# Block 2's mixers: the value projection of each head pair one pair later

## The chip, the cores and the metric

The kernel runs on one core of one Trainium2 chip. The metric is the device time of one execution in microseconds (us). Before the change it is 3103.43 us, the median of three runs (3101.84 to 3103.62).

## The reference, cut to what matters

Two blocks of two layers each work on a stream of 512 tokens of width 1024 in f32. The change concerns the mixers of the second block: in each, one projection gives queries, keys and values, 8 pairs of heads attend, and an output projection follows.

```python
def dilated_attention_mixer(u, w_in, w_out, cos, sin):          # block 2, layer 0: "mixer 1"
    q, k, v = jnp.split(u @ w_in, 3, axis=-1)
    q = apply_partial_rope(split_heads(q, A_HEADS), cos, sin)   # 16 heads of 64: 8 head pairs
    k = apply_partial_rope(split_heads(k, A_HEADS), cos, sin)
    v = split_heads(v, A_HEADS)
    ...
        o, lse = banded_attention(by_residue(q)[..., None, :, :], by_residue(k), by_residue(v),
                                  radius, A_BLOCK)
    ...
    w = jax.nn.softmax(jnp.stack(lses), axis=0)
    o = jnp.einsum('pbhs,pbhsd->bhsd', w, jnp.stack(outs))
    return merge_heads(o).astype(u.dtype) @ w_out

def differential_attention_mixer(u, w_in, w_out, lam_q1, ..., sub_g, cos, sin, layer_idx):   # layer 1: "mixer 2"
    q, k, v = jnp.split(u @ w_in, 3, axis=-1)
    ...
        p = jax.nn.softmax(sc, axis=-1)
        a = p[:, :, 0] - lam * p[:, :, 1]
        return jnp.einsum('bhqk,bhkd->bhqd', a.astype(v.dtype), v, preferred_element_type=f32)
    ...
    o = rms_norm(o, sub_g) * (1.0 - lam_init)
    return merge_heads(o).astype(u.dtype) @ w_out
```

A pair of heads (two of 64 in mixer 1, the two halves of one head in mixer 2) needs 128 columns of q, of k and of v: 24 column tiles in all.

## The kernel before, in words

All is written out by hand: each engine has its own program, and semaphores tie them together. A **unit** is one column tile of a weight, 1024 x 128, times all 512 tokens. SyncE loads its weight in the order of the list `stream()`, ScalarE makes `w_hi` of it (L1470), VectorE the rest `w_lo` (L2194), four units ahead at most (`SLOTS`), and TensorE then runs 8 x 3 matmuls (L569: hi by hi, lo by hi, hi by lo). In the mixers a unit is cut into two **halves** of 12 matmuls (`half(0)`, `half(1)`), which stand between the steps of the attention.

The function `fused(l)` is the mixer, and exists once for each engine; l is 0 for mixer 1 and 1 (`diff`) for mixer 2. The units come as q0 k0 v0, q1 k1 v1, ... Pass r of the loop (1 to 8) does the attention of pair r-1 while it projects pair r; the last pass has nothing to project. In a pass, for each of four blocks of 128 queries:

- `score(p, q)` (L1139), TensorE: two scores of 512 keys. It waits until the exponentials of the score before it are done, and score 0 until q and k of its pair have been rotated (`f_roped`).
- `maxima` (L2800 in mixer 1, L2798 in mixer 2), VectorE; `exps` (L1974), ScalarE; `normalise` (L2808 to L2817), VectorE.
- `turn(p, q)` (L1150), TensorE: the probabilities transposed; `copies` (L1983), ScalarE.
- `values(r)` (L1172), TensorE: the pair's v, evicted to `y`, is transposed into bank `F_R`; ScalarE copies it to `v` (L2014).
- `outputs(p)` (L1164, L1160 in mixer 2), TensorE: probabilities times v, one pass later; `take` (L2821), VectorE, brings them to `o`.

The rotation of the next pair's q and k is spread over the pass: `evict` (L2786, L2788), `rope_sin` (L2827, L2829: a shuffle through the same bank `F_R`, times the sine), the product with the cosine on GpSimd (L3123), and `rope_add` (L2835).

Where TensorE would have nothing to do, `kept_busy` (L596) issues matmuls whose result nobody reads: six in pass 1 and groups of three in the last pass. In the last pass the output projection begins as well (`out_begun`, L569, into banks 0 and 1): its operand `a_hi`, `a_lo` is made of `o` by ScalarE (`out_rounded`, L1830) and VectorE (`out_low`, L2239). Mixer 2 first applies a norm to `o`: `norm_spread` (L1214), TensorE, into banks 0 and 1, free once all 24 units are evicted, and `norm_applied` (L2855), VectorE.

Of the kernel before, what the change touches and what calls it, by code (L numbers as in the profile page):

```python
# [26 lines left out]
P = 128  # L27
# [50 lines left out]

def stream():

    order, at = [], 0
    for _ in range(LAYERS):
        order += [(at + j, 8) for j in range(WIN_T + 8)]
        order += [(at + WIN_T + 72, 0), (at + WIN_T + 76, 0)]
        order += [(at + WIN_T + 8 + j, 8) for j in range(64)]
        order += [(at + WIN_T + 80 + j, 8) for j in range(8)]
        at += WIN_T + 88
    for _ in range(LAYERS):
        order += [(at + 8 * part + r, 8) for r in range(8) for part in range(3)]
        order += [(at + 24 + j, 8) for j in range(8 + 16 + 8 + 8 + 24 + 24 + 12)]  # L90
        order += [(at + 124 + j, 6) for j in range(8)]
        at += 132
    return order
# [110 lines left out]
def build(nc, dram, out):  # L204
    ctx = ExitStack()
    with ctx:
# [268 lines left out]
        def _(pe):  # L475
# [632 lines left out]
            def fused(l):  # L1108
# [59 lines left out]
                def values(r):  # L1168
                    pe.wait_ge(bank_free, first + 3 * r + 3)
                    pe.wait_ge(f_sin, 2 * (pairs + r + 1) + (1 if r + 1 < PAIRS else 0))  # L1170
# [55 lines left out]
                for r in range(1, PAIRS + 1):  # L1226
                    more = r < PAIRS
                    if more:
                        half(0)
                    if r == 1:  # L1230
                        kept_busy(F_O, 6, 2 * P)
                    score(r - 1, 0)
                    if r >= 2:
                        outputs(r - 2)
                    if more:
                        half(1)
                    score(r - 1, 1)
                    turn(r - 1, 0)
                    if more:
                        half(0)  # L1240
                    else:
                        kept_busy(W_BANK[0] if diff else F_R, 3, 2 * P)
                    score(r - 1, 2)
                    if not more and diff:
                        norm_spread(0)
                        norm_spread(1)
                    turn(r - 1, 1)
                    if more:
                        half(1)
                    else:  # L1250
                        kept_busy(F_R, 3, 2 * P)
                    score(r - 1, 3)
                    if not more:
# [3 lines left out]
                        else:  # L1257
                            kept_busy(F_R, 3, 2 * P)
                            out_begun((0, 1))
                    turn(r - 1, 2)  # L1260
                    values(r - 1)
                    if more:
                        half(0)
                    elif diff:
                        pe.wait_ge(f_copied, turns(l, PAIRS) - 2)
                        kept_busy(F_T[1], 4, 2 * P)
                        norm_spread(4)
                        norm_spread(5)
                        kept_busy(F_T[1], 1, 2 * P)
                    else:  # L1270
                        out_begun((2, 3))
# [3 lines left out]
                    if more:  # L1275
# [180 lines left out]
        def _(act):  # L1456
# [505 lines left out]
            def fused(l):  # L1962
# [60 lines left out]
                for r in range(1, PAIRS + 1):  # L2023
                    last = r == PAIRS
                    ahead(first + 3 * r + 2 if not last else first + 3 * r + 1)
                    exps(r - 1, 0)
                    if not last:
                        ahead(first + 3 * r + 3)
# [8 lines left out]
                    else:  # L2037
                        ahead(first + 3 * r + 4)
# [3 lines left out]
                    values(r - 1)  # L2042
# [139 lines left out]
        def _(dve):  # L2182
# [594 lines left out]
            def fused(l):  # L2777
# [45 lines left out]
                def rope_sin(r, k):  # L2823
                    if k == 1 and r > 0:
                        dve.wait_ge(f_v_ready, pairs + r)
# [46 lines left out]
                for r in range(1, PAIRS + 1):  # L2872
                    more = r < PAIRS
                    if more:
                        ahead(first + 3 * r + 2)
# [5 lines left out]
                    normalise(r - 1, 0)  # L2881
                    if r >= 2:
                        take(r - 2)
                    if more:
                        evict(r, 0)
                    maxima(r - 1, 1)
                    if more:
                        ahead(first + 3 * r + 3)
# [4 lines left out]
                    maxima(r - 1, 2)  # L2893
                    if more:
# [16 lines left out]
                    if more:  # L2911
                        rope_sin(r, 1)
                        ahead(first + 3 * r + 4)
                        rope_add(r, 1)
                        evict(r, 2)
# [341 lines left out]
```

## Time and profile before

| | us |
|---|---|
| median of three runs | 3103.43 |
| the profiled execution | 3101.19 |
| its span | 3099.4 |
| TensorE busy with matmuls | 3042.0 (98%) |
| VectorE busy | 1754.2 (57%) |
| ScalarE busy | 1254.4 (40%) |
| GpSimd busy | 297.7 (10%) |

Mixer 1's eight passes run from 1430.92 to about 1657 us of the span, mixer 2's from 2271.61 to about 2503 us. The share of a busy engine is an average over the whole span; what a pass waits for is read in its own timeline, where a row in square brackets says how long the engine stood idle and what released it.

### The profile page before, as it was taken

What the parts mean: (1) busy time and instruction counts of PE and PEld (TensorE: products, weight loads), DVE (VectorE), ACT (ScalarE), POOL (GpSimd) and SP (SyncE); (2) the same over time, 40 slices, a digit from 0 to 9 for tenths busy, and PEclk for the clock granted to TensorE, in tenths of its full rate; (3) what the DMA queues carried; (4) which work ended last, traced back from release to release, by engine and by line L of the source; (5) the groups of instructions that cost most, each with busy time, mean ns of one, the idle gap of its engine ahead of it and who ended that gap; (6) DMA issues with size and microseconds to landing.
All of it is one profiled execution on the core that took longest, in us unless ns stands there. A gap on an engine that the chain in (4) does not pass through costs nothing.

```text
span 3099.4 us, 38484 instructions
## 1 busy us (share of the span) xinstructions
PE 3042.0 (98%) x15248; PEld 2422.4 (78%) x15248; DVE 1754.2 (57%) x2564; ACT 1254.4 (40%) x2084; POOL 297.7 (10%) x257
## 2 busy tenths in 40 slices
PE   7999999999999999999999999999999999999998
PEld 6777888887777888887667878888866678788886
DVE  7755644357656544467775635344577755354444
ACT  6644323245544322344444534232344444342322
POOL 2011100011011100011001102000110010020001
PEclk9999999999999999999999999999999999999999
DMA  3111233332111333332112322233211133223332
GB/s 139 55 49 60 93 100 95 95 96 86 56 42 66 95 96 101 95 95 74 55 55 89 122 68 82 95 98 100 89 60 56 48 95 112 65 89 97 101 95 82
DMA packets 73726, 259.14 MB, mean 84 GB/s; under 512 B 8020, under 2 KB 10200, under 8 KB 73176
## 3 DMA queue, kind: packets, MB, share of 16 engines
q1 hardware_dynamic: 72824, 252.99, 26.1%
q0 software_dynamic: 736, 3.87, 0.4%
q8 instruction: 113, 1.85, 0.2%
q14 instruction: 53, 0.43, 0.0%
HBM read 254.73 MB, written 2.10 MB: 83 GB/s over the span
## 4 chain that ended last, share of the span: by engine, by line
PE 84%; issue 6%; DVE 6%; ACT 1%; POOLq 1%; DVEq 1%; DMA 0%; POOL 0%; ACTq 0%
PE bank L569 68%; PE bank L499 2%; PE bank L1139 1%; POOLq L3081 1%; PE bank L793 1%; DVE w_lo L2194 1%; PE bank L1150 1%; PE bank L1364 1%; PE bank L1343 1%; PE bank L1094 1%; PE bank L1160 1%; PE bank L1164 1%; PE bank L823 0%; PE bank L836 0%; DMA w_raw<-weights 0%
## 5 line engine op out<-in xcount | busy, mean ns | idle before, releaser
L569 PE MATMUL bank<-a_hi,w_hi 128*128 128x512 f32 x2120 | 848.1, 400 | 19.3 <-DVE w_lo L2194 15.1
L569 PE MATMUL bank<-a_hi,w_lo 128*128 128x512 f32 x2120 | 828.6, 391 | 0.0
L569 PE MATMUL bank<-a_lo,w_hi 128*128 128x512 f32 x2120 | 827.4, 390 | 0.0
L2194 DVE TENSOR_TENSOR w_lo<-w_raw,w_hi 128x1024 fp32r<-128x1024 f32 (+1 forms) x474 | 612.2, 1293 | 285.4 <-ACT w_hi L1470 283.7
L1470 ACT ACTIVATE w_hi<-w_raw 128x1024 fp32r<-128x1024 f32 (+1 forms) x474 | 494.8, 1045 | 417.1 <-DMA w_raw<-weights 417.1
L569 PE MATMUL bank<-b_hi,w_hi 128*128 128x512 f32 (+1 forms) x1516 | 572.9, 378 | 2.6 <-DVE w_lo L2194 1.5
L569 PE MATMUL bank<-b_lo,w_hi 128*128 128x512 f32 (+1 forms) x1516 | 564.2, 372 | 0.0
L569 PE MATMUL bank<-b_hi,w_lo 128*128 128x512 f32 (+1 forms) x1516 | 564.0, 372 | 0.0
L569 PEld LDWEIGHTS bank<-a_hi,w_hi 128*128 128x128 f32 x2120 | 399.3, 188 | 120.0 <-issue 21.7
L569 PEld LDWEIGHTS bank<-a_hi,w_lo 128*128 128x128 f32 x2120 | 399.0, 188 | 85.6
L569 PEld LDWEIGHTS bank<-a_lo,w_hi 128*128 128x128 f32 x2120 | 399.6, 189 | 83.2 <-issue 3.8
L569 PEld LDWEIGHTS bank<-b_hi,w_hi 128*128 128x128 f32 x1516 | 286.2, 189 | 63.4 <-issue 9.7
L569 PEld LDWEIGHTS bank<-b_hi,w_lo 128*128 128x128 f32 x1516 | 286.3, 189 | 50.2
L569 PEld LDWEIGHTS bank<-b_lo,w_hi 128*128 128x128 f32 x1516 | 286.5, 189 | 49.9 <-issue 1.7
L3080 POOL TENSOR_TENSOR sq_sum<-sq_sum,sq 128x512 f32<-128x512 f32 (+1 forms) x119 | 160.6, 1349 | 322.1 <-ACT sq L1523 317.7
L1974 ACT ACTIVATE prob<-bank,der 128x512 f32<-128x512 f32 x128 | 87.0, 685 | 207.8 <-DVE der L2800 108.4
L3078 POOL COPY sq_sum<-sq 128x512 f32<-128x512 f32 (+1 forms) x18 | 11.5, 639 | 1580.9 <-ACT sq L1523 1580.9
L2604 DVE TENSOR_TENSOR x<-x,bank 128x512 f32<-128x512 f32 x80 | 55.0, 687 | 179.6 <-PE bank L569 179.6
L1867 ACT ACTIVATE y<-y 128x512 f32<-128x512 f32 x64 | 40.4, 632 | 219.7 <-DVE y L2642 219.7
L2140 ACT ACTIVATE b_hi<-y 128x512 fp32r<-128x512 f32 x44 | 27.8, 632 | 189.1 <-DVE y L3033 189.1
L3039 DVE TENSOR_TENSOR y<-y,bank 128x512 f32<-128x512 f32 x46 | 31.6, 688 | 119.1 <-PE bank L569 119.1
L2239 DVE TENSOR_TENSOR b_lo<-y,b_hi 128x512 fp32r<-128x512 f32 x76 | 52.7, 693 | 69.7 <-ACT b_hi L1868 39.0
(341 smaller groups left out, 3172.5 us busy)
## 6 DMA issues: line engine op xcount, KB each, us to landing
w_raw<-weights SPq DMA_DIRECT2D x458, 512.0 KB, 3.5
w_raw<-weights SPq DMA_DIRECT2D x16, 384.0 KB, 3.0
x<-x SPq DMA_DIRECT2D x8, 256.0 KB, 7.4
mem<-mem POOLq DMA_DIRECT2D x2, 1024.0 KB, 5.3
out<-x SPq DMA_DIRECT2D x8, 256.0 KB, 2.1
mem<-mem SPq DMA_DIRECT2D x1, 1024.0 KB, 12.4
ple<-ple POOLq DMA_DIRECT2D x2, 512.0 KB, 4.0
o<-c_level SPq DMA_DIRECT2D x1, 512.0 KB
```

The source lines that it names most:

```text
L499: last = mm(bank[unit_bank(u) if at is None else at][:, hs(e)], w[:, u % SLOTS, ks], t[:, k, hs(e)], start=(k == 0 and n == 0), stop=(k == ...
L569: last = mm(bank[unit_bank(u) if at is None else at][:, 0:cols], w[:, u % SLOTS, ks], t[:, k, 0:cols], start=(k == begun and n == 0), stop ...
L793: last = mm(bank[2 + 2 * p + e][:, cols], k_, q_, start=True, stop=True)
L1094: last = mm(bank[b][:, :], w[:, u % SLOTS, ks], t[:, k, :], start=(k == 0 and i == 0), stop=(k == 1 and i == 2))
L1470: f(w_hi[:, u % SLOTS, 0:widths[u]], w_raw[:, u % SLOTS, 0:widths[u]], ACT.Copy).then_inc(w_hi_ready, 1)
L1867: f(y[:, 20 + j % 2, :], y[:, 16 + j % 2, :], ACT.Square)
L1974: f(prob[:, i % 4, :], bank[F_S[e]][:, :], ACT.Exp, bias=stat_n[:, i % 8:i % 8 + 1], scale=1.0 if diff else -1.0, accum_out=stat_d[:, i % ...
L2194: tt(w_lo[:, u % SLOTS, w], w_raw[:, u % SLOTS, w], f32(w_hi[:, u % SLOTS, w]), ALU.subtract).then_inc(w_lo_ready, 1)
L2239: tt(h[1][:, k, :], src, f32(h[0][:, k, :]), ALU.subtract).then_inc(h_ready, 1)
L2604: tt(x[:, k, :], x[:, k, :], b[:, :], ALU.add).then_inc(bank_free, 1)
L3039: step(lambda u, b: tt(y[:, k, :], y[:, k, :], b[:, :], ALU.add).then_inc(bank_free, 1))
L3080: pool.tensor_tensor(sq_sum[:, 0:cols], sq_sum[:, 0:cols], s, ALU.add).then_inc(sq_added, 1)
```

## The change

In both mixers q and k keep their places, and each v but the first is projected one pass later: the order becomes q0 k0 v0, q1 k1, q2 k2 v1, ..., q7 k7 v6, v7. Pass 1 projects q1, k1 and the first half of q2, and pass 2 begins with its score at once, without a half ahead of it. The last pass has the two halves of v7. `values` moves from the end of its pass to the place behind the first score of the next, `outputs` from behind the first score to behind the second, `take` from ahead of the second maxima to behind them. Of the groups of three `kept_busy` matmuls in the last pass, two go in mixer 1 and two in mixer 2; in mixer 2 the first two `norm_spread` now come behind the second turn. The weight splits (`ahead`) of pass 1 become one fewer and the last pass has one more.

```diff
@@ the order of the weights
+MIX_ORDER = [(0, 0), (1, 0), (2, 0), (0, 1), (1, 1)]
+MIX_ORDER += [u for r in range(2, 8) for u in ((0, r), (1, r), (2, r - 1))] + [(2, 7)]
...
-        order += [(at + 8 * part + r, 8) for r in range(8) for part in range(3)]
+        order += [(at + 8 * part + r, 8) for part, r in MIX_ORDER]
...
@@ TensorE
                 def values(r):
-                    pe.wait_ge(bank_free, first + 3 * r + 3)
-                    pe.wait_ge(f_sin, 2 * (pairs + r + 1) + (1 if r + 1 < PAIRS else 0))
+                    pe.wait_ge(bank_free, first + MIX_ORDER.index((2, r)) + 1)
+                    pe.wait_ge(f_sin, 2 * (pairs + min(r + 2, PAIRS)))
+                    if r == PAIRS - 1:
+                        pe.wait_ge(f_v_ready, pairs + r)
...
                 for r in range(1, PAIRS + 1):
                     more = r < PAIRS
-                    if more:
+                    if r == 1:
                         half(0)
-                    if r == 1:
                         kept_busy(F_O, 6, 2 * P)
+                    elif r > 2 and more:
+                        half(0)
                     score(r - 1, 0)
                     if r >= 2:
+                        values(r - 2)
+                    half(1 if more else 0)
+                    score(r - 1, 1)
+                    if r >= 2:
                         outputs(r - 2)
-                    if more:
-                        half(1)
-                    score(r - 1, 1)
                     turn(r - 1, 0)
-                    if more:
-                        half(0)
-                    else:
-                        kept_busy(W_BANK[0] if diff else F_R, 3, 2 * P)
+                    half(0 if more else 1)
                     score(r - 1, 2)
-                    if not more and diff:
-                        norm_spread(0)
-                        norm_spread(1)
                     turn(r - 1, 1)
                     if more:
                         half(1)
+                    elif diff:
+                        norm_spread(0)
+                        norm_spread(1)
                     else:
+                        pe.wait_ge(f_v_ready, pairs + PAIRS - 1)
                         kept_busy(F_R, 3, 2 * P)
                     score(r - 1, 3)
...
-                            kept_busy(F_R, 3, 2 * P)
                             out_begun((0, 1))
                     turn(r - 1, 2)
-                    values(r - 1)
                     if more:
                         half(0)
...
                     turn(r - 1, 3)
-                    if more:
+                    if more and r > 1:
                         half(1)
...
@@ ScalarE
-                    ahead(first + 3 * r + 2 if not last else first + 3 * r + 1)
+                    ahead(first + (5 if r == 1 else 3 * r + 1))
                     exps(r - 1, 0)
+                    if r >= 2:
+                        values(r - 2)
                     if not last:
-                        ahead(first + 3 * r + 3)
+                        ahead(first + (6 if r == 1 else 3 * r + 2))
...
@@ VectorE
                 def rope_sin(r, k):
-                    if k == 1 and r > 0:
-                        dve.wait_ge(f_v_ready, pairs + r)
+                    if k == 0 and r > 1:
+                        dve.wait_ge(f_v_ready, pairs + r - 1)
...
                     normalise(r - 1, 0)
+                    if more:
+                        evict(r, 0)
+                    maxima(r - 1, 1)
                     if r >= 2:
                         take(r - 2)
                     if more:
-                        evict(r, 0)
-                    maxima(r - 1, 1)
-                    if more:
-                        ahead(first + 3 * r + 3)
+                        ahead(first + (6 if r == 1 else 3 * r + 2))
                     normalise(r - 1, 1)
...
                     maxima(r - 1, 2)
+                    if not more:
+                        evict(r - 1, 2)
...
                         rope_sin(r, 1)
-                        ahead(first + 3 * r + 4)
+                        if r > 1:
+                            ahead(first + 3 * r + 3)
                         rope_add(r, 1)
-                        evict(r, 2)
+                        if r > 1:
+                            evict(r - 1, 2)
```

Three places show the new order. Line numbers of the changed kernel are 4 higher on TensorE up to L1150, where they were, 6 higher behind it, and 8 higher on VectorE. The first place is TensorE at the end of pass 1 of mixer 1; L569 or L573 and a line of dots is a half of 12 matmuls (in the last but one row before, of 24). Before:

```order
L1139 MATMUL bank<-y 128x512 x2
L1150 MATMUL bank<-small,prob 128x128 x8
L1172 MATMUL bank<-small,y 128x128 x4
L569 MATMUL bank<-a_hi,w_hi 128x512
...
L1150 MATMUL bank<-small,prob 128x128 x8
L569 MATMUL bank<-a_hi,w_hi 128x512
...
L1139 MATMUL bank<-y 128x512 x2
L1164 MATMUL bank<-prob_t,v 64x512 x8
```

And now:

```order
L1143 MATMUL bank<-y 128x512 x2
L1154 MATMUL bank<-small,prob 128x128 x8
L573 MATMUL bank<-a_hi,w_hi 128x512
...
L1154 MATMUL bank<-small,prob 128x128 x8
L1143 MATMUL bank<-y 128x512 x2
L1178 MATMUL bank<-small,y 128x128 x4
```

The last turn of pass 1 (L1154) and the first score of pass 2 (L1143) are now neighbours, where two halves lay between, and the transposed values (L1178) stand behind that score.

The second place is TensorE in the last pass of mixer 2, from the second score on (L1150 is a turn, L596 the `kept_busy` group, L1214 two `norm_spread`). Before:

```order
L1139 MATMUL bank<-y 128x512 x2
L1150 MATMUL bank<-small,prob 128x128 x4
L596 MATMUL bank<-small 128x256 x3
L1139 MATMUL bank<-y 128x512 x2
L1214 MATMUL bank<-small,g_r 128x128 x8
L1150 MATMUL bank<-small,prob 128x128 x4
L596 MATMUL bank<-small 128x256 x3
L1139 MATMUL bank<-y 128x512 x2
L1214 MATMUL bank<-small,g_r 128x128 x8
L1150 MATMUL bank<-small,prob 128x128 x4
L1172 MATMUL bank<-small,y 128x128 x4
```

And now (the half in it is the second of v7):

```order
L1143 MATMUL bank<-y 128x512 x2
L1164 MATMUL bank<-prob_t,v 128x512 x4
L1154 MATMUL bank<-small,prob 128x128 x4
L573 MATMUL bank<-a_hi,w_hi 128x512
...
L1143 MATMUL bank<-y 128x512 x2
L1154 MATMUL bank<-small,prob 128x128 x4
L1220 MATMUL bank<-small,g_r 128x128 x8
L1143 MATMUL bank<-y 128x512 x2
L1220 MATMUL bank<-small,g_r 128x128 x8
L1154 MATMUL bank<-small,prob 128x128 x4
L1178 MATMUL bank<-small,y 128x128 x4
```

Both groups of three are gone, a half stands in the place of the first, and the first spreads come behind the turn and right ahead of the fourth score.

The third place is VectorE in the same pass (L2821 is `take`, L2840 the clamp of the norm, L2798 maxima, L2855 two `norm_applied`). Before:

```order
L2821 COPY o<-bank 128x512
L2798 TENSOR_REDUCE der<-bank 128x1 x2
L2808 RECIPROCAL der<-der 128x2
L2812 TENSOR_SCALAR prob<-prob,der 128x512
L2814 SCALAR_TENSOR_TENSOR prob<-prob,der 128x512
L2840 TENSOR_SCALAR y<-o 128x512
L2798 TENSOR_REDUCE der<-bank 128x1 x2
L2855 SCALAR_TENSOR_TENSOR o<-bank,vec,o 128x512 x2
```

And now:

```order
L2806 TENSOR_REDUCE der<-bank 128x1 x2
L2829 COPY o<-bank 128x512
L2816 RECIPROCAL der<-der 128x2
L2820 TENSOR_SCALAR prob<-prob,der 128x512
L2822 SCALAR_TENSOR_TENSOR prob<-prob,der 128x512
L2848 TENSOR_SCALAR y<-o 128x512
L2806 TENSOR_REDUCE der<-bank 128x1 x2
L2796 TENSOR_TENSOR y<-bank,r_x 128x512
L2863 SCALAR_TENSOR_TENSOR o<-bank,vec,o 128x512 x2
```

The copy of the outputs stands behind the maxima, and the eviction of v7 (L2796) ahead of the norm.

## Rows read from the trace of the kernel before

**Rows 1.** The page, sections 1 and 5: busy us; a group: busy us, mean ns, idle.

```profile
PE 3042.0 (98%) x15248; PEld 2422.4 (78%) x15248; DVE 1754.2 (57%) x2564; ACT 1254.4 (40%) x2084; POOL 297.7 (10%) x257
...
L2194 DVE TENSOR_TENSOR w_lo<-w_raw,w_hi 128x1024 fp32r<-128x1024 f32 (+1 forms) x474 | 612.2, 1293 | 285.4 <-ACT w_hi L1470 283.7
```

**Rows 2.** TensorE's waits: line, releaser, us in total, times, longest.

```profile
PE bank L1139 <- DVE y L2835: 2.1, 3, 1.1
...
PE bank L569 <- DVE o L2855: 0.8, 1, 0.8
```

**Rows 3.** Pass 2, mixer 1; passes 2 and 8, mixer 2: stretch, length, busy, clock.

```profile
1456.25:1485.13 28.88, 28.88 (x141) 19.23 (x140) 20.34 (x43) 13.14 (x28) 2.59 (x2) 1.00 0.18 56
...
2296.26:2324.47 28.21, 27.95 (x125) 18.83 (x124) 21.72 (x36) 11.99 (x26) 2.60 (x2) 1.00 0.18 55
...
2463.21:2502.82 39.61, 36.49 (x173) 24.30 (x173) 24.04 (x47) 16.70 (x36) 0.59 (x1) 1.00 0.12 41
```

**Rows 4.** Timeline, mixer 1, passes 1 and 2: start, us, engine, line; idle before.

```profile
1446.62 0.60 PE L1172 MATMUL bank<-small,y 128*128 128x128 f32 x4
...
1449.83 1.04 PE L1150 MATMUL bank<-small,prob 128*128 128x128 f32 x8
...
1456.25 1.13 PE L1139 MATMUL bank<-y 64*128 64x512 f32 x4
...
1460.89 0.50 PE L569 MATMUL bank<-a_hi,w_hi 128*128 128x512 f32 x1
...
1461.01 0.69 DVE L2821 COPY o<-bank 128x512 f32<-128x512 f32 x1 [0.20 <-PE bank L1164]
...
1463.84 1.13 PE L1139 MATMUL bank<-y 64*128 64x512 f32 x4
```

**Rows 5.** Timeline, VectorE and GpSimd, end of pass 1, mixer 1: the rotation.

```profile
1450.09 1.29 POOL L3123 TENSOR_TENSOR y<-y,cos_t 128x512 f32<-128x512 f32 x1 [5.54 <-DVE bank L2827]
...
1450.71 1.75 DVE L2194 TENSOR_TENSOR w_lo<-w_raw,w_hi 128x1024 fp32r<-128x1024 f32 x1
1452.38 0.68 DVE L2835 TENSOR_TENSOR y<-y,f_t 128x512 f32<-128x512 f32 x1
```

**Rows 6.** Timeline, TensorE, last pass of mixer 1.

```profile
1633.48 1.46 PE L596 MATMUL bank<-small 128*128 128x256 f32 x6
...
1638.40 1.13 PE L1139 MATMUL bank<-y 64*128 64x512 f32 x4
...
1641.65 0.47 PE L569 MATMUL bank<-a_hi,w_hi 128*128 128x512 f32 x1 [0.64 <-DVE a_lo L2239]
```

**Rows 7.** Timeline, TensorE and GpSimd, passes 1 and 2 of mixer 2.

```profile
2290.19 0.66 PE L1150 MATMUL bank<-small,prob 128*128 128x128 f32 x4 [0.48 <-DVE prob L2814]
...
2291.03 1.30 POOL L3123 TENSOR_TENSOR y<-y,cos_t 128x512 f32<-128x512 f32 x1 [6.34 <-DVE bank L2827]
...
2296.26 1.13 PE L1139 MATMUL bank<-y 64*128 64x512 f32 x4
...
2313.93 0.66 PE L1150 MATMUL bank<-small,prob 128*128 128x128 f32 x4 [0.27 <-DVE prob L2814]
```

**Rows 8.** Timeline, VectorE and TensorE, last pass of mixer 2.

```profile
2471.29 1.13 PE L1139 MATMUL bank<-y 64*128 64x512 f32 x4 [0.37 <-ACT prob L1974]
...
2473.32 1.28 DVE L2798 TENSOR_REDUCE der<-bank 128x1 f32<-128x512 f32 x2
2474.52 1.40 DVE L2855 SCALAR_TENSOR_TENSOR o<-bank,vec,o 128x512 f32<-128x512 f32 x2
2475.84 0.16 DVE L2808 RECIPROCAL der<-der 128x2 f32<-128x2 f32 x1
...
2477.36 1.28 DVE L2798 TENSOR_REDUCE der<-bank 128x1 f32<-128x512 f32 x2
...
2485.47 0.47 PE L569 MATMUL bank<-a_hi,w_hi 128*128 128x512 f32 x1 [0.77 <-DVE o L2855]
```

**Rows 9.** Timeline and windows, TensorE in block 1: a stretch at half clock.

```profile
70.83 0.63 PE L569 MATMUL bank<-a_hi,w_lo 128*128 128x512 f32 x1
...
72.00:74.00 2.00, 2.00 (x6) 1.41 (x6) 1.82 (x2) 1.94 (x3) 0.00 (x0) 0.50 0.00 0
```

More of the change, by code:

```diff
@@ L1257, in fused @@
                         else:
-                            kept_busy(F_R, 3, 2 * P)
                             out_begun((0, 1))
                     turn(r - 1, 2)
-                    values(r - 1)
                     if more:
                         half(0)
[L1264 to L1269, printed above, removed]
-                    else:
-                        out_begun((2, 3))
+                    else:
+                        values(r - 1)
+                        if diff:
+                            pe.wait_ge(f_copied, turns(l, PAIRS) - 2)
+                            kept_busy(F_T[1], 4, 2 * P)
+                            norm_spread(4)
+                            norm_spread(5)
+                            kept_busy(F_T[1], 1, 2 * P)
+                        else:
+                            out_begun((2, 3))
                     if diff and more and r >= 2:
@@ L2036, in fused @@
                         out_rounded((0, 1))
-                    else:
-                        ahead(first + 3 * r + 4)
+                    elif r > 1:
+                        ahead(first + 3 * r + 3)
                     exps(r - 1, 3)
@@ L2041, in fused @@
                         out_rounded((2, 3))
-                    values(r - 1)
+                        values(r - 1)
                     copies(r - 1, 2)
@@ L2873, in fused @@
                     more = r < PAIRS
-                    if more:
-                        ahead(first + 3 * r + 2)
+                    ahead(first + (5 if r == 1 else 3 * r + 1))
                     if l == 0 and r == 1:
@@ L2884, in fused @@
                     if more:
-                        evict(r, 0)
-                    maxima(r - 1, 1)
-                    if more:
-                        ahead(first + 3 * r + 3)
+                        ahead(first + (6 if r == 1 else 3 * r + 2))
                     normalise(r - 1, 1)
@@ L2912, in fused @@
                         rope_sin(r, 1)
-                        ahead(first + 3 * r + 4)
+                        if r > 1:
+                            ahead(first + 3 * r + 3)
                         rope_add(r, 1)
-                        evict(r, 2)
+                        if r > 1:
+                            evict(r - 1, 2)
                     else:
```

## The prediction

> **What bounds the kernel now.** I read the page first: TensorE is busy for 98% of the span [rows 1]. A gain must therefore take time out of TensorE's own row: matmuls, or waits. The table of TensorE's waits comes next: the lines of the mixers stand there with 2.1 us in three waits and 0.8 us in one [rows 2], so there is little idle time to recover, and what matters is whether the change makes new waits. Third the stretches: pass 2 of mixer 1 is 28.88 us with TensorE busy for all 28.88; pass 2 of mixer 2 is 28.21 us, busy for 27.95, with VectorE at 21.72 [rows 3]. In the last pass of mixer 2 (39.61 us up to the unbroken output products) TensorE is busy for 36.49. Last the timelines around the places that move: the reader should ask at each what the wait behind the moved work is anchored to.
>
> **The change part by part.** Nothing is computed less: 48 units, 16 values, 16 outputs. Only four groups of three filler matmuls go, at 1.46 us [rows 6]: 5.84 us. That is the whole of what can be won on TensorE; the rest is where two halves per mixer (12 matmuls each) lie. They leave the end of pass 1 and go to the last pass. I follow each mixer from its first score; T is the start of a pass's first score.
>
> *Mixer 1, pass 1 to 2.* Before, the values start at 1446.62, the last turn at 1449.83, the next T is 1456.25 [rows 4]. Now the values go (about 0.4 us: four transposes), the turn starts near 1449.4, and TensorE is free for the score at 1450.4. But the score needs the rotated k1, and that chain hangs on pass 1's fourth normalisation, not on TensorE: behind it the shuffle, the cosine product on GpSimd 1450.09 plus 1.29 gives 1451.38, then the addition, 0.68 [rows 5]. Before, a weight split (1450.71, 1.75 us) put the addition off to 1452.38, under cover of the two halves; that split now moves to pass 2, so the addition can begin at 1451.4 and end at 1452.1. T moves from 1456.25 to 1452.15: 4.1 us earlier, not the 6 us of work that left, and TensorE idles for 1.8 us.
>
> *Mixer 1, passes 2 to 7.* The same work in another order; pass 2 was full [rows 3]. The new places need a check of three waits. (a) Outputs wait for the copy of v: the copy, 0.6 us, follows the first exponentials, the second score waits for those same exponentials and takes 1.06 us, and outputs stand behind it: covered. (b) `take` now blocks VectorE behind the second maxima until the outputs end: in the trace it starts 3.70 us behind their start (1461.01 against T+1.06) [rows 4], so at T+9.1. Behind it are queued the take (0.7), a split (1.3 [rows 1]) and the second normalisation (1.5, from 2475.84 to 2477.36 [rows 8]): done at T+12.6. The turn that needs it now stands at about T+13.3 in mixer 2 and T+13.8 in mixer 1, since outputs and values came in front of it. Cover 0.7 and 1.2 us. (c) The new weight order keeps the distance of four units. I take 0 us, with bounds of -0.2 and +0.2 a pass from transitions between kinds of matmul.
>
> *Mixer 1, last pass.* In front of its last score stand two halves more (1460.89 to 1463.84: 2.95 each [rows 4]) and one more set of values (0.4), and one filler group less (1.46, and its transition): +4.7 us. The second filler group that goes stood behind that score, 1638.40, and the output product behind it began at 1641.65, released by VectorE's `a_lo` [rows 6]: 3.25 us behind the score. That distance is VectorE's (maxima, then `a_lo`) and stays. So taking the filler away gives nothing there; it turns into idle time of 2.2 us. Sum +4.7. Mixer 1 together: -4.1 + 4.7 = +0.6 us.
>
> *Mixer 2, pass 1 to 2.* Here even the last turn waits for VectorE (2290.19, idle 0.48) [rows 7], so the values that leave ahead of it give nothing: it stays at 2290.19. GpSimd's product ends at 2292.33 [rows 7], the addition 0.7 later, T = 2293.1 instead of 2296.26: -3.2 us, with 2.2 us idle.
>
> *Mixer 2, passes 2 to 7.* Each pass has a wait for VectorE of 0.27 us ahead of its third turn [rows 7]. From the third score to the fourth turn VectorE's chain is the longer one; the values that stood between the third and fourth turn covered 0.4 us of it, and in front of the third score they now lengthen TensorE's part. So of the 0.4 us only 0.3 come back: +0.12 a pass, +0.7 us for six. Bounds: 0 (all comes back) and +0.4 (nothing does), that is 0 to 2.4 us.
>
> *Mixer 2, last pass.* VectorE decides. Before, T is 2463.21, the third score 2471.29, its maxima 2473.32, the output product starts at 2485.47 on VectorE's last `norm_applied`: 12.15 us of VectorE work behind those maxima, T+22.3 [rows 3, 8]. Now the third score comes at T+12.3 (was T+8.1: two halves and values more, 6.3, one filler group, the idle 0.37 and transitions less), its maxima 1.15 later at T+13.5. Then VectorE has to evict v7 (0.6, a 128x512 operation like the take), and only that frees banks 0 and 1 for `norm_spread`, which was issued early before and now starts behind it: about 0.7 us of transposes until `norm_applied` can go (estimate: four transposes are 0.66 in rows 7, and half of the eight must be through). Then the 12.15: T+27.0. That is +4.7 (27.0 less 22.3), and of the two filler groups, 2.9 us, nothing reaches the end. Bounds: +4.0 (the spread is hidden) to +5.5 (both spreads count).
>
> Mixer 2 together: -3.2 + 0.7 + 4.7 = +2.2 us. Behind the output product's start nothing changes in either mixer.
>
> *Sum.* 0.6 + 2.2 = +2.8, say +2.9 us with the roundings. Against the profiled execution, 3101.19 us (span 3099.4), that is 3104.1; that execution lies 2.24 us under the median of the three runs, 3103.43, so I expect a median of 3106.3 us, +0.1%.
>
> **The rivals.**
>
> *A, the fillers were the price.* If VectorE's chains shrink or slide so that no new wait appears, the 5.84 us come out whole: 3097.6 us. For it: mixer 1's full passes, TensorE 28.88 of 28.88. Against it: the output product is released by VectorE in both last passes already before the change [rows 6, 8], and the rotation cannot be had earlier than its input. A partial form (one mixer) gives about 3101.
>
> *B, the clock falls in the new gaps, the case that ends slower.* The trace has such falls: after 4 us of matmuls on four rows, the granted clock stands at 0.50 of full, the lower level of 1.2 GHz, in the window 72 to 74 us, and seven products from 70.83 on take 0.43 us apart instead of 0.23 [rows 9]: 1.4 to 1.7 us a fall. The new gaps are up to 2.2 us, and the longest in a mixer before was 1.1, without a fall [rows 2]; so the trace doesn't say what 2.2 do. There are five places: two in mixer 1 (1.8, 2.2), the front of mixer 2 (2.2), and two or three in its last pass, where the fillers go as well. One fall gives 3107.9, two 3109.5; from the third on it is over 0.2% slower, 3111.1. Against it: around each gap TensorE is at full work, and the filler of six matmuls in pass 1 and the other groups near the end stay.
> The Trainium skill ("TensorE: Matmul & The Clock Gate", "HAM oscillation — how this bites in real kernels") says that waits of TensorE can bring its half-rate clock back, so that a loop with short work between waits pays at every round. By it removing fillers is a risk and not a gain; the falls in block 1 agree that it happens in this kernel, and no row shows it for a gap of this size.
>
> *C, the take holds up normalisation.* If outputs end a microsecond later for VectorE than I count, the second turn of each pass of mixer 2 waits: the cover of 0.7 us is used up, then each tenth costs 0.6 us over six passes, in mixer 1 from 1.2 us on. At 0.5 us over it: 3.0 us more, 3109.3.
>
> **How the numbers follow.** Chances: forecast 0.62 (3103.5 to 3108), A in full or in part 0.15, B with one or two falls 0.11 and with three or more 0.06, C 0.06. The range that should hold 8 in 10 reaches down to 3100 (a partial A) and up to 3110.5 (two falls and a little), which takes in the bounds: the low ends (-1.2 for passes 2 to 7 of mixer 1, -0.7 for mixer 2's, -0.7 for the spread) sum to 3103.7, the high ones (+1.2, +1.7, +0.8) to 3110.0. A difference of 0.2%, 6.2 us, is about what a measurement of this kernel can tell from none. Slower than 3109.6: B from three falls, a part of two falls and of C: 0.12. Faster than 3097.2: only A and something more: 0.04. Within: 0.84.
>
> **What the profile would show.** Right: TensorE idle for some 1.8 and 2.2 us ahead of the second pass's first score in the two mixers, released by the addition of the rotation; the output products starting about 3.25 us behind the last score in mixer 1 with some 2 us idle, and some 27 us behind the first score of the last pass in mixer 2, on `norm_applied`; passes 2 to 7 as long as before within 0.2 us. Wrong: a first score of pass 2 that is 6 us earlier, an output product released by TensorE's own queue, waits ahead of the second turn (C), or a granted clock under 1.00 between 1430 and 1700 or 2270 and 2550 us (B).

## The result, and the profile after

The changed kernel takes 3110.34 us, the median of 11 runs (3106.71 to 3115.94); the kernel before, on the same chip, 3103.62 us (11 runs, 3101.68 to 3110.32). The ratio is 1.0023, with an interval of 1.0015 to 1.003: slower, by some 7 us, where the forecast had the change 2.9 us slower. The forecast median of 3106.3 us is 4.0 us too low; the measured time lies at the upper end of the range. The profiled execution took 3108.76 us with a span of 3106.9, 7.5 us more than the span before.

The page, section 1: busy time of each engine. TensorE has the busy time that it had [rows 1], although the twelve filler matmuls (four groups of three; the trace counts each as two) went.

```profile
PE 3042.1 (98%) x15224; PEld 2421.1 (78%) x15224; DVE 1751.9 (56%) x2564; ACT 1256.1 (40%) x2084; POOL 298.4 (10%) x257
```

TensorE's waits: line, releaser, us in total, times, longest (L1143 is a score, L1154 a turn, L573 the projections, L1220 `norm_spread`; `outputs` are L1168 in mixer 1 and L1164 in mixer 2, 4 lines behind their old places and not 6).

```profile
PE bank L1143 <- DVE y L2843: 6.1, 5, 2.2
PE bank L1154 <- DVE prob L2822: 3.6, 10, 0.9
...
PE bank L573 <- DVE a_lo L2247: 2.1, 1, 2.1
...
PE bank L1220 <- DVE y L2796: 1.5, 1, 1.5
```

The score's wait for the rotation was 2.1 us in three [rows 2] and is 6.1 in five. The turn's was 2.7 us in nine, the longest 0.5. The one for `a_lo` was 1.1 us in two, the longest 0.6 [rows 6], and is now one of 2.1; the `norm_spread` of 1.5 is new.

Stretches: pass 2 of mixer 1; passes 2 and 3 of mixer 2; its last pass up to the unbroken output products. Length, then busy us of each engine, and the granted clock after POOL.

```profile
1452.45:1481.27 28.82, 28.82 (x141) 19.18 (x141) 21.50 (x44) 13.24 (x28) 2.58 (x2) 1.00 0.15 51
2294.30:2325.41 31.11, 30.72 (x124) 20.39 (x124) 22.93 (x37) 12.09 (x26) 2.59 (x2) 0.91 0.17 47
2325.41:2353.91 28.50, 28.11 (x125) 18.86 (x125) 21.77 (x36) 12.09 (x26) 2.59 (x2) 1.00 0.17 56
2465.71:2510.42 44.71, 40.85 (x188) 27.84 (x189) 26.14 (x49) 18.60 (x38) 0.59 (x1) 0.97 0.14 48
```

Against [rows 3], pass 2 of mixer 1 is the same, and the last pass of mixer 2 is 5.1 us longer. The pass that stands out is pass 2 of mixer 2: 31.11 us against 28.21, and against 28.50 in the next pass, which does the same work. Its clock is the only one of the four at 0.91.

The front of mixer 1, TensorE's timeline (start, us, engine, line; idle before and its releaser), and VectorE's:

```profile
1449.70 1.04 PE L1154 MATMUL bank<-small,prob 128*128 128x128 f32 x8
1452.45 1.13 PE L1143 MATMUL bank<-y 64*128 64x512 f32 x4 [1.71 <-DVE y L2843]
```

```profile
1451.70 0.69 DVE L2843 TENSOR_TENSOR y<-y,f_t 128x512 f32<-128x512 f32 x1 [0.59 <-POOL y L3134]
1452.40 1.23 DVE L2202 TENSOR_TENSOR w_lo<-w_raw,w_hi 128x1024 fp32r<-128x1024 f32 x1
```

Two halves fewer stand between the turn and the score, and TensorE waits 1.71 us for the rotation's addition. The weight split (L2202), which stood ahead of the addition [rows 5], is behind it. The end of mixer 1:

```profile
1639.31 1.13 PE L1143 MATMUL bank<-y 64*128 64x512 f32 x4
1642.57 0.47 PE L573 MATMUL bank<-a_hi,w_hi 128*128 128x512 f32 x1 [2.13 <-DVE a_lo L2247]
```

The output product begins 3.26 us behind the last score, as before (3.25, [rows 6]), with 2.13 us idle where the filler group was. The front of mixer 2:

```profile
2291.41 0.66 PE L1154 MATMUL bank<-small,prob 128*128 128x128 f32 x4 [0.93 <-DVE prob L2822]
2294.30 2.08 PE L1143 MATMUL bank<-y 64*128 64x512 f32 x4 [2.23 <-DVE y L2843]
2296.30 1.11 PE L1178 MATMUL bank<-small,y 128*128 128x128 f32 x4
2297.07 0.77 PE L573 MATMUL bank<-a_hi,w_hi 128*128 128x512 f32 x1
```

Here two gaps follow each other, 0.93 and 2.23 us, with one turn between them. Behind the second the same score that took 1.13 us [rows 7] takes 2.08, and the matmuls of the half are longer too. The stretches of 2 us say why:

```profile
2290.00:2292.00 2.00, 1.07 (x7) 0.48 (x5) 1.82 (x4) 0.20 (x1) 0.00 (x0) 1.00 0.00 0
2292.00:2294.00 2.00, 0.07 (x1) 0.00 (x0) 1.31 (x3) 1.54 (x2) 1.27 (x1) 0.77 0.00 0
2294.00:2296.00 2.00, 1.71 (x4) 0.50 (x4) 1.38 (x2) 0.00 (x0) 0.00 (x0) 0.50 0.00 0
2296.00:2298.00 2.00, 2.00 (x8) 1.58 (x7) 1.29 (x2) 0.87 (x3) 0.00 (x0) 0.50 0.00 0
2298.00:2300.00 2.00, 2.00 (x6) 1.54 (x5) 1.24 (x3) 2.00 (x4) 0.00 (x0) 0.52 0.00 0
```

The granted clock falls in the gap, from 1.00 to 0.50 of full (1.2 instead of 2.4 GHz), and stays there until about 2299.9, 5.6 us behind the gap's end. Worked out from the clock of the windows, it had fallen at about 2293.1, 1.0 us into the second wait, and the stretch at half clock is 6.8 us. The last pass of mixer 2:

```profile
2481.17 1.06 PE L1220 MATMUL bank<-small,g_r 128*128 128x128 f32 x8 [1.47 <-DVE y L2796]
...
2492.79 0.47 PE L573 MATMUL bank<-a_hi,w_hi 128*128 128x512 f32 x1 [0.77 <-DVE o L2863]
```

`norm_spread` waits 1.47 us for the eviction of v7 (L2796), and the output product begins 27.08 us behind the first score (2465.71); before it was 22.26 [rows 3, 8].

The account of the mixers from these rows, T being the start of a pass's first score:

| term | forecast | trace |
|---|---|---|
| mixer 1, pass 1 | -4.1 | -4.14 (21.19 for 25.33) |
| mixer 1, passes 2 to 7 | 0 | -0.04 |
| mixer 1, last pass | +4.7 | +4.73 |
| mixer 2, pass 1 | -3.2 | -3.19 (21.46 for 24.65) |
| mixer 2, passes 2 to 7 | +0.7 | +1.85, and 2.61 at half clock |
| mixer 2, last pass | +4.7 | +4.82, and 0.28 behind the output product |

The rows give 0.6 us for mixer 1 and 6.4 for mixer 2. Behind mixer 2's last row here, up to the next block's first sum of squares (2510.42 to 2550.01, before 2502.82 to 2541.82), are 0.6 us more. The spans differ by 7.5. The rest nearly cancels and lies in stretches that the change doesn't touch: mixer 1 begins 0.3 us later (1431.26 for 1430.92), another 0.3 come in between the mixers (mixer 2 begins 1.23 us later), and behind 2550 us this execution gains 0.7 on the one before.

At the end of mixer 2 the clock is under 1.00 too. In order: two windows; TensorE's timeline there (L1202 sums over one column, L600 filler, L573 the unbroken products); the same product in e3, a run described below, which has the same code from the last pass on and no fall:

```profile
2500.00:2510.00 10.00, 9.64 (x51) 7.92 (x50) 3.54 (x8) 2.14 (x5) 0.59 (x1) 0.91 0.30 107
2510.00:2520.00 10.00, 10.00 (x43) 8.21 (x42) 6.19 (x8) 4.33 (x7) 1.89 (x2) 0.92 0.27 105
```

```profile
2504.51 1.84 PE L1202 MATMUL bank<-der,y 128*128 128x1 f32 x16
...
2508.21 2.77 PE L600 MATMUL bank<-small 128*128 128x256 f32 x6
2510.42 0.99 PE L573 MATMUL bank<-a_hi,w_hi 128*128 128x512 f32 x1
```

```profile
2510.29 0.50 PE L573 MATMUL bank<-a_hi,w_hi 128*128 128x512 f32 x1 [0.50 <-DVE a_lo L2249]
```

From the output product's start to this one are 17.63 us here, 17.34 in e3 (27.11 and 44.45 behind the pass's first score, 2465.84) and 17.35 before: the 0.28 us are that fall's. The filler takes 2.77 us for 1.46, and the first product 0.99 for 0.50.

### The profile page after: what moved, and what is told of

Its sections match the earlier page's. It is cut to its first block, busy times and chain, and to the rows that moved or that the text cites. A ratio compares the mean times of both kernels' runs of the same rounds, so it can differ in the third digit from the quotient of the medians.

```text
span 3106.9 us, 38436 instructions
## 1 busy us (share of the span) xinstructions
PE 3042.1 (98%) x15224; PEld 2421.1 (78%) x15224; DVE 1751.9 (56%) x2564; ACT 1256.1 (40%) x2084; POOL 298.4 (10%) x257
## 3 DMA queue, kind: packets, MB, share of 16 engines
q8 instruction: 113, 1.85, 0.2%
## 4 chain that ended last, share of the span: by engine, by line
PE 83%; issue 7%; DVE 5%; ACT 1%; POOLq 1%; DVEq 1%; DMA 0%; POOL 0%; ACTq 0%
PE bank L573 68%; PE bank L503 2%; PE bank L1143 2%; POOLq L3092 1%; PE bank L797 1%; DVE w_lo L2202 1%; PE bank L1154 1%; PE bank L1370 1%; PE bank L1349 1%; PE bank L1098 1%; PE bank L1164 1%; PE bank L1168 1%; PE bank L827 0%; PE bank L840 0%; DMA w_raw<-weights 0%
## 5 line engine op out<-in xcount | busy, mean ns | idle before, releaser
L573 PE MATMUL bank<-a_hi,w_hi 128*128 128x512 f32 x2120 | 847.4, 400 | 20.6 <-DVE w_lo L2202 15.3
L573 PE MATMUL bank<-a_hi,w_lo 128*128 128x512 f32 x2120 | 829.3, 391 | 0.0
L573 PE MATMUL bank<-a_lo,w_hi 128*128 128x512 f32 x2120 | 828.1, 391 | 0.0
L2202 DVE TENSOR_TENSOR w_lo<-w_raw,w_hi 128x1024 fp32r<-128x1024 f32 (+1 forms) x474 | 612.2, 1293 | 288.4 <-ACT w_hi L1476 286.9
L573 PE MATMUL bank<-b_hi,w_hi 128*128 128x512 f32 (+1 forms) x1516 | 572.9, 378 | 2.1 <-DVE w_lo L2202 0.9
L573 PE MATMUL bank<-b_lo,w_hi 128*128 128x512 f32 (+1 forms) x1516 | 564.0, 372 | 0.0
L573 PE MATMUL bank<-b_hi,w_lo 128*128 128x512 f32 (+1 forms) x1516 | 564.0, 372 | 0.0
L573 PEld LDWEIGHTS bank<-a_hi,w_hi 128*128 128x128 f32 x2120 | 400.0, 189 | 115.1 <-DVE w_lo L2202 17.6
L573 PEld LDWEIGHTS bank<-a_hi,w_lo 128*128 128x128 f32 x2120 | 399.6, 188 | 85.8
L573 PEld LDWEIGHTS bank<-a_lo,w_hi 128*128 128x128 f32 x2120 | 400.2, 189 | 82.1 <-issue 2.4
L573 PEld LDWEIGHTS bank<-b_hi,w_hi 128*128 128x128 f32 x1516 | 286.2, 189 | 62.8 <-issue 10.1
L573 PEld LDWEIGHTS bank<-b_lo,w_hi 128*128 128x128 f32 x1516 | 286.6, 189 | 50.0 <-issue 1.7
L573 PEld LDWEIGHTS bank<-b_hi,w_lo 128*128 128x128 f32 x1516 | 286.3, 189 | 50.2
```

The lines of the kernel that those rows point to most:

```text
L573: last = mm(bank[unit_bank(u) if at is None else at][:, 0:cols], w[:, u % SLOTS, ks], t[:, k, 0:cols], start=(k == begun and n == 0), stop ...
L2202: tt(w_lo[:, u % SLOTS, w], w_raw[:, u % SLOTS, w], f32(w_hi[:, u % SLOTS, w]), ALU.subtract).then_inc(w_lo_ready, 1)
```

## The experiments

Kernels of one group ran on one chip beside the kernel before: e1 to e4 beside 33 runs of it (median 3103.43 us, 3101.15 to 3108.68), e5 to e8 beside 27 (3103.61 us, 3101.82 to 3108.55). Each of e1 to e7 ran 11 times, e8 once. The changed kernel itself didn't run in these groups; its 3110.34 us are compared through the ratios.

**e1 and e2: one mixer changed, the other as before.** The edit, with `fused_old` the functions of the kernel before; in e2 it is `(1,)`. An edit moves the line numbers below it, here and in e3, e6 and e7:

```diff
-        order += [(at + 8 * part + r, 8) for part, r in MIX_ORDER]
+        order += [(at + 8 * part + r, 8) for part, r in
+                  (MIX_ORDER if l in (0,) else
+                   [(part, r) for r in range(8) for part in range(3)])]
...
-                fused(l)
+                (fused if l in (0,) else fused_old)(l)
```

> Mixer 1 with the new order, mixer 2 as before. Theory W+C (new waits on VectorE, and on top a fall of TensorE's clock in mixer 2 alone): mixer 1 from its first score to its unbroken output products takes 0.6 us more than before (front 4 us earlier, last pass 4.7 us longer), its gaps of 1.7 and 2.1 us keep the clock at 1.00, and the kernel is 0.6 us slower, 1.0002. Rival W (waits alone, spread over both mixers): half of the 7 us, +3 us or 1.001.

Measured: 3107.30 us (3102.50 to 3108.77), ratio 1.0006 (0.9997 to 1.0015). Mixer 1 shows the passes of the changed kernel (21.19, 28.89, last 26.18) and both gaps, 1.71 and 2.13 us, at a clock of 1.00; mixer 2 those of before (24.60, 28.22). No difference can be told in the time, as the account says (+0.6); but the interval holds the rival's 1.001 as well, so it is the passes of the trace that decide for 0.6. The median lies 3.9 us above that of the kernel before. In the profiled execution (3108.47 us) the excess lies ahead of the mixers: mixer 1 begins at 1437.40 instead of 1430.92, with more of block 1 at half clock (one stretch, before and here):

```profile
150.00:160.00 10.00, 10.00 (x74) 8.17 (x73) 6.04 (x11) 3.43 (x5) 0.00 (x0) 0.87 0.17 54
```

```profile
150.00:160.00 10.00, 10.00 (x49) 8.00 (x49) 4.06 (x9) 3.67 (x5) 0.00 (x0) 0.67 0.00 0
```

> Mixer 2 with the new order, mixer 1 as before. Theory W+C: +6.4 us (front -3.2, passes 2 to 7 +1.9 for waits and +2.6 for the clock, last pass +4.8, rest the clock's second fall), 1.002, with the clock under 0.8 in the ten us behind the first gap. Rival W: +3 to +4 us and, if the clock falls, then with no more than 0.5 us behind it.

Measured: 3108.17 us (3106.36 to 3111.37), ratio 1.0017 (1.0008 to 1.0026): slower. Pass 2 of mixer 2 is 30.09 us, passes 3 to 6 are 28.48 or 28.49. The two gaps (0.92 and 2.23 us) stand at the same place, and the clock falls again; the windows are 2290 to 2310 us of e2:

```profile
2290.00:2300.00 10.00, 6.85 (x27) 4.17 (x27) 7.76 (x13) 4.04 (x8) 1.27 (x1) 0.84 0.10 39
2300.00:2310.00 10.00, 10.00 (x38) 6.14 (x37) 5.88 (x10) 4.36 (x11) 0.00 (x0) 0.99 0.18 54
```

The loss is mixer 2's: the passes show it, and the interval of e2 is clear of 1 where that of e1 is not.

**e3: the changed kernel with a filler in the front gap of mixer 2.** Four filler matmuls, which the trace shows as eight, ahead of pass 2's first score:

```diff
                     elif r > 2 and more:
                         half(0)
+                    elif r == 2 and diff:
+                        kept_busy(F_O, 4, 2 * P)
```

> The changed kernel with four filler matmuls (1.9 us) in mixer 2 ahead of pass 2's first score, inside the idle time of 2.2 us. Theory W+C: the score starts where it did (within 0.1 us), the clock stays at 1.00 in 2290 to 2300 us, pass 2 takes 28.5 us instead of 31.1, and the kernel is 2.6 us faster than the changed one (some +4 to +5 us over the kernel before, 1.0014). Rival W: pass 2 and the time stay as they are, +7 us, since a filler does no work.

Measured: 3107.08 us (3105.01 to 3112.21), ratio 1.0012 (1.0003 to 1.0021). TensorE's timeline, and the window:

```profile
2294.21 0.66 PE L1154 MATMUL bank<-small,prob 128*128 128x128 f32 x4 [0.93 <-DVE prob L2824]
2294.71 1.89 PE L600 MATMUL bank<-small 128*128 128x256 f32 x8
2297.11 1.13 PE L1143 MATMUL bank<-y 64*128 64x512 f32 x4 [0.51 <-DVE y L2845]
```

```profile
2290.00:2300.00 10.00, 8.56 (x42) 6.20 (x43) 8.21 (x14) 4.48 (x10) 1.28 (x1) 1.00 0.11 46
```

The score still waits for the same addition, pass 1 is as long (21.48 us), but TensorE has work in the gap, the clock stays at 1.00, the score takes 1.13 us and pass 2 takes 28.50. That is 2.61 us less than in the changed kernel. Matmuls whose result nobody reads give it back: the clock is the cause of these 2.6 us, not the wait. The times alone couldn't show it, since the interval overlaps the changed kernel's (1.0015 to 1.003). The end of mixer 2 shows 1.00 here as well.

**e4: the missing half later.** In the changed kernel two halves are missing at the end of pass 1. Here one of them is put back there, and one is missing at the end of pass 2, in both mixers:

```diff
-                    elif r > 2 and more:
-                        half(0)
+                    elif more:
+                        half(1 if r == 2 else 0)
...
-                    if more and r > 1:
+                    if more and r > 2:
                         half(1)
```

with the numbers of the halves between them exchanged in pass 2.

> The changed kernel with one half of a unit back between pass 1's last turn and pass 2's first score, and the second half missing at the end of pass 2 instead, in both mixers. Theory W+C: in mixer 1 no idle time at either place, 1.7 us won; in mixer 2 pass 2's first score 0.4 us later than in the changed kernel, an idle time of some 0.4 us ahead of pass 3, 1.8 us won, and no fall of the clock there, 2.6 us; together 6 us less than the changed kernel, +1 us over before, 1.0003. Rival W: 3.5 us less, +3.5 us over before, 1.001. A third one, that the loss is in the last passes alone: no gain, since these are not touched.

Measured: 3104.71 us (3101.61 to 3111.33), ratio 1.0007 (0.9998 to 1.0016). Passes 1 and 2 are 22.17 and 26.18 us in mixer 1, 21.91 and 26.29 in mixer 2: together 48.35 and 48.20 us, against 54.21 and 52.86 before and 50.01 and 52.57 in the changed kernel. In mixer 1 that is 5.86 us for the two halves, all that they cost. The front's waits are gone, and with them the fall in mixer 2. But now the other new gap has one, at the end of mixer 1:

```profile
1637.31 1.13 PE L1143 MATMUL bank<-y 64*128 64x512 f32 x4
1640.57 0.77 PE L573 MATMUL bank<-a_hi,w_hi 128*128 128x512 f32 x1 [2.13 <-DVE a_lo L2247]
1641.13 0.63 PE L573 MATMUL bank<-a_lo,w_hi 128*128 128x512 f32 x1
1641.56 0.63 PE L573 MATMUL bank<-a_hi,w_lo 128*128 128x512 f32 x1
```

```profile
1640.00:1650.00 10.00, 9.43 (x45) 7.96 (x46) 4.48 (x9) 4.76 (x11) 0.00 (x0) 0.83 0.00 0
```

The products start 0.43 us apart instead of 0.23, and the unbroken ones begin at T+36.91 where the changed kernel had T+35.41 with the clock at 1.00: this fall costs 1.5 us. The same gap of 2.13 us had no fall in the changed kernel.

**e5: the eviction of v7 ahead of the third maxima.**

```diff
-                    maxima(r - 1, 2)
                     if not more:
                         evict(r - 1, 2)
+                    maxima(r - 1, 2)
```

> The changed kernel with v7's eviction ahead of the last pass's third maxima on VectorE instead of behind them. Theory W (VectorE's chain from the third maxima to the output product decides mixer 2's last pass): the wait of 1.47 us ahead of the first norm_spread goes, the output product starts 25.8 us behind the pass's first score instead of 27.1, and in mixer 1 nothing moves; 1.3 us less than the changed kernel. Rival (TensorE's added halves decide): the output product stays at 27.1 us.

Measured: 3108.36 us (3106.20 to 3111.37), ratio 1.0017 (1.0008 to 1.0026). TensorE's timeline in the last pass of mixer 2:

```profile
2482.76 1.04 PE L1220 MATMUL bank<-small,g_r 128*128 128x128 f32 x8
...
2494.55 0.47 PE L573 MATMUL bank<-a_hi,w_hi 128*128 128x512 f32 x1 [0.80 <-DVE o L2863]
```

`norm_spread` doesn't wait, and the output product begins 25.61 us behind the first score (2468.94) instead of 27.08: 1.47 us, the whole of that wait. The chain that the forecast laid on VectorE is shown by this; 1.5 us is too little to be told in the time, whose interval overlaps the changed kernel's. The front gap is unchanged, and pass 2 is 29.98 us at a clock of 0.93 and 0.90 in its two windows.

**e6: the half of e4, the eviction of e5, and a filler in the last gap of mixer 1.**

```diff
                         else:
+                            kept_busy(F_R, 3, 2 * P)
                             out_begun((0, 1))
```

> The hole moved as in e4, v7's eviction early as in e5, and one filler group (1.46 us) back behind mixer 1's last score. By the traces: against the kernel before, mixer 1 -5.9 us over passes 1 and 2 and +4.7 in the last pass, mixer 2 -4.7, +1.5 over passes 3 to 7 and +3.5: together -0.9 us, if no clock falls in the mixers; 0.9997, not to be told from 1. Rival (something outside the mixers costs as well): over 1.0005.

Measured: 3102.21 us (3098.79 to 3104.56), ratio 0.9993 (0.9984 to 1.0002). Its interval lies wholly under the changed kernel's, and it holds 1: no difference to the kernel before. The gap behind mixer 1's last score is filled, and the clock is 1.00 at the three places where it had fallen:

```profile
1640.06 1.13 PE L1143 MATMUL bank<-y 64*128 64x512 f32 x4
1641.12 1.56 PE L600 MATMUL bank<-small 128*128 128x256 f32 x6
```

```profile
2290.00:2300.00 10.00, 9.08 (x43) 6.22 (x43) 7.21 (x13) 5.10 (x11) 1.30 (x1) 1.00 0.17 52
2500.00:2510.00 10.00, 9.14 (x48) 7.36 (x48) 6.72 (x11) 4.75 (x8) 0.61 (x1) 1.00 0.21 78
1640.00:1650.00 10.00, 9.36 (x46) 7.05 (x46) 5.96 (x15) 6.82 (x16) 0.00 (x0) 1.00 0.00 0
```

From first score to the last pass's, mixer 1 gains 5.87 us against before (190.06 for 195.93) and mixer 2 gains 3.17 (188.43 for 191.60). Mixer 2's last pass gives 3.34 back up to the output product (25.60 for 22.26), and mixer 1's takes 4.73 more, as in the changed kernel (unbroken products at T+35.41, before T+30.68). None of the orders tried did better: the halves taken from the front are paid in the last pass.

**e7: the kernel before without its four filler groups.** The groups that the change takes out, and nothing else:

```diff
                     if more:
                         half(0)
-                    else:
-                        kept_busy(W_BANK[0] if diff else F_R, 3, 2 * P)
                     score(r - 1, 2)
...
-                    else:
+                    elif not diff:
                         kept_busy(F_R, 3, 2 * P)
...
-                            kept_busy(F_R, 3, 2 * P)
                             out_begun((0, 1))
```

> The kernel before, without the four filler groups that the change takes away (two in each mixer's last pass), all else as before. Theory W+C: each was under a wait for ScalarE or VectorE, so scores and output products stay within 0.3 us of where they were, TensorE is idle for 5.8 us more, and what can change is the clock: 0 to two falls of 1.3 to 2.6 us. Rival A (the fillers are a price): 5.8 us faster, 0.998.

Measured: 3103.65 us (3101.98 to 3107.68), ratio 1.0003 (0.9993 to 1.0012). The scores of the last passes stand where they did (T+4.65, +8.10, +11.55 in mixer 1), with idle time in the fillers' place. The first two rows are mixer 1's, the third the end of mixer 2 in windows:

```profile
1638.27 1.13 PE L1139 MATMUL bank<-y 64*128 64x512 f32 x4 [1.30 <-ACT prob L1971]
...
1644.98 0.47 PE L569 MATMUL bank<-a_hi,w_hi 128*128 128x512 f32 x1 [2.13 <-DVE a_lo L2236]
```

```profile
2500.00:2510.00 10.00, 9.64 (x48) 8.15 (x47) 5.74 (x10) 3.52 (x6) 0.00 (x0) 0.83 0.22 89
```

Taking out the 5.84 us of filler gave nothing: rival A is false at its root.

**e8: the kernel before in another execution**, to see what of a trace comes again. No edit.

> The kernel before once more, for a second trace. If the spread of its runs (3101 to 3109 us) comes from where the clock falls in block 1, this trace shows other stretches under 1.00 there than the first one, and the mixers' passes within 0.1 us of the first trace.

Measured: 3103.98 us. The passes agree within 0.05 us (25.30, 28.89, 24.62, 28.21). What differs is block 1, where the same stretch had 0.83:

```profile
840.00:850.00 10.00, 10.00 (x57) 8.52 (x57) 4.45 (x9) 5.45 (x7) 0.00 (x0) 0.66 0.14 53
```

## Why the prediction was right in its waits and wrong in its time

- *What bounds the kernel, and the fronts.* Right. The first scores of pass 2 wait for the rotation, 1.71 and 2.23 us (forecast 1.8 and 2.2), and come 4.14 and 3.19 us earlier (4.1 and 3.2).
- *Mixer 1, passes 2 to 7.* Right; neither turn nor outputs wait. Rival C, a turn held up by the take, doesn't appear: no second turn waits. In a full pass of mixer 2 the timeline marks only the wait ahead of the third turn, 0.26 us, as before.
- *The last passes.* Right: 3.26 us from last score to output product in mixer 1, T+27.08 in mixer 2 (forecast 3.25 and T+27.0), both on the operand named. e5 and e7 show that VectorE's chains set both.
- *Mixer 2, passes 2 to 7.* The mechanism was right and the size wrong: +1.85 us where +0.7 was forecast (bounds 0 to 2.4). The rows are the third and fourth turn of pass 3 (T 2325.41), then the fourth before (T 2324.47):

```profile
2343.50 0.66 PE L1154 MATMUL bank<-small,prob 128*128 128x128 f32 x4 [0.26 <-DVE prob L2822]
...
2347.84 0.66 PE L1154 MATMUL bank<-small,prob 128*128 128x128 f32 x4
```

```profile
2346.63 0.63 PE L1150 MATMUL bank<-small,prob 128*128 128x128 f32 x4
```

  The third turn comes 0.42 us later than before (T+18.09 for T+17.67), the time of the values now ahead of it. Its wait of 0.26 didn't shrink, since VectorE's maxima hang on a third score that is as much later. The fourth comes 0.27 later (T+22.43 for T+22.16). I had let 0.3 of the 0.4 us come back; only 0.15 did, and a pass is 0.29 us longer. Pass 7 is 0.42 longer, as the last pass's first score waits 0.45 us for the rotation, 0.31 before. The upper bound would have been the better value, since no row showed slack behind that turn.
- *The failed step: rival B.* The forecast put the clock's price into its sum at nothing and gave it a chance of 0.17, with the argument that "around each gap TensorE is at full work". That was false at the front of mixer 2, where half clock cost 2.6 us. There the gap was not the 2.2 us of the forecast alone: the turn ahead of it already waited (0.48 us before, 0.93 now), and TensorE was idle for 3.16 of the 3.82 us up to the score. The row of the first wait stood in [rows 7], and I used it only to place the turn. The fall came in each of the three traces with this pair of gaps (the changed kernel, e2, e5) and in none of those where the second gap was filled (e3) or didn't arise (e1, e4, e6). That the first wait was needed for it is argued, not shown: no run filled the first alone, and in e4 one wait of 2.13 us was enough. For it speaks that in the changed kernel the clock was down 1.0 us into the second wait, while the whole 1.71 us at mixer 1's front left it at 1.00 in four traces.
- *The price of a fall.* Also too low: 1.4 to 1.7 us from block 1 [rows 9], measured 2.6 here, 1.6 in e2 (30.09 less 28.49), 1.5 in e5 and 1.5 in e4. It goes with the length of the stretch at half clock: worked out from the windows, 3.4 us in e2 (0.84 and 0.99), in e5 (0.93 and 0.90) and in e4 (0.83), 6.8 in the changed kernel, of which 1.2 were idle. The rest caught the score, the values and the first six matmuls of the half. e3 shows the 2.6 us by taking them back.

The Trainium skill ("TensorE: Matmul & The Clock Gate", "HAM oscillation — how this bites in real kernels") tells of a kernel whose waits are longer than the short work between them, so that each wait brings the half-rate clock back. The trace agrees in kind: one turn between waits of 0.93 and 2.23 us, and then a clock of 0.50.

The sum with what was measured: 2.8 forecast for the mixers, 2.6 of clock in pass 2, 1.15 in passes 2 to 7, 0.12 and 0.28 in the last pass of mixer 2 make 6.95, and the 0.6 us behind it 7.55. The medians differ by 6.7. That the spans differ by 7.5 as well is in part luck, since the 0.3 and 0.3 us ahead of mixer 2 and the 0.7 gained at the end are not in this sum. The waits and the 2.6 us of clock explain the loss; the last few tenths of a us can't be told.

What stays open: why the clock falls at the end of mixer 2 in the changed kernel, e2 and e7 (0.91, 0.92 and 0.83) and not in e1, e3 to e6 and e8. The one-column sums, the spread and the fillers ahead of it are the same in all. e3 prices the 0.28 us, and the 0.6 behind it fit the first products, which still meet half clock (the second and third start 0.79 and 1.18 us behind the first, at full clock 0.33 and 0.56), but no run removed this fall by an edit. Nor was it tried to run the changed kernel beside e3, so the 3.3 us between their medians rest on two chips; the 2.6 within them rest on the traces.

## What to carry to other kernels

Before judging that the clock holds in a new wait, look at what TensorE does just ahead of it: where a wait and a short piece of work stand there, add that wait to the new one (three traces of three with such a pair had a fall, though no run shows that both waits were needed). Price the fall by what runs at half clock, not by the gap. Work moved out of a stretch that ends on another engine's chain leaves idle time and gives only the part down to that chain; put one piece less there and take the second from a full stretch, as e4 does. And a filler in a wait cost nothing here (e7) and was once worth 2.6 us (e3).

## What the runs showed of the hardware that I had not expected

- The length of a gap alone doesn't decide: 2.13 us at the end of mixer 1 kept the clock at 1.00 in the changed kernel, e1, e3, e5 and e7, and was followed by half clock in e4 (0.83 over 10 us). The 1.71 us at its front had no fall in any of the four traces that show it. What decides between such cases stays open.
- At the end of mixer 2 the clock can be under 1.00 with TensorE busy for 9.64 of 10 us (0.91 in the changed kernel, 0.83 in e7), and be 1.00 with less (e6: 9.14). The busy share of a stretch doesn't tell the kind of work: ahead of the changed kernel's fall stand 16 matmuls of one column each, 1.84 us; they stand in e6 as well, where no fall follows.
- Block 1's falls differ between executions of one kernel: 0.83 and 0.66 in the same stretch. Mixer 1's first score, ahead of which every kernel here does the same work, begins between 1430.92 (before, e4) and 1437.40 us (e1). So a difference of a few us between two spans can lie wholly in front of what was changed, and the passes are to be compared from their own first score. The times go with the clock too: of the changed kernel, those with a mean granted clock of 0.992 took 3113.95 us or more, the one with 0.995 took 3106.71. The Trainium skill ("TensorE: Matmul & The Clock Gate", "What's actually happening") says that the point at which the clock rises at a kernel's start varies from run to run; the traces show such a variation in the middle of one.
